# RWKV-7 heads of a diffusion trunk: the state chain of one turn interleaved with the token turns and gram blocks of the next

## The chip, the cores and the metric

The kernel runs on one core of a Trainium2 chip: TensorE (matmul), VectorE, ScalarE, GpSimd and SyncE (whose queue issues the DMAs) work in parallel and synchronise through semaphores. Matmuls write to PSUM, which has eight banks of 128 partitions x 512 fp32. The metric is the device time of one execution of the whole program in microseconds, lower is better.

## The reference

Two layers of a trunk over 256 latent and 256 context tokens, 1024 wide. Each layer projects its input, runs three token mixers (Mamba-2, RWKV-7, neighbourhood attention), merges them, and ends in a mixture of experts. The change is in the RWKV-7 mixer only: 16 heads of 64, both directions, context first, its final state the latent tokens' initial one. With `S` a 64 x 64 state per head:

```
w = -softplus(-(w0 + tanh(wl) @ w2)) - 0.5;  decay = exp(-exp(w))
a = sigmoid(a0 + al @ a2);  g = sigmoid(gl) @ g2
kk = unit(k * k_k);  k_dir = k * (1 + (a - 1) * k_a)
def step(S, inp):
    s_kk = S @ kk_t
    S = S * w_t - outer(s_kk, kk_t * a_t) + outer(v_t, k_t)
    return S, S @ r_t
y = y_forward + flip(y_backward)
out = (groupnorm(y) * ln_w + ln_b + sum(r * k_b * r_k) * v) * g
```

## The kernel before

`rwkv_heads` does this chunked. The 512 tokens are eight chunks of 64. The 1024 channels are done in eight turns of 128 channels (two heads `h`, on partition halves; both directions `z` together). `mix(b, c, ...)` is turn b; c is the next turn, whose features are prepared meanwhile. There is one `mix` for each engine, and each runs its own list in program order; the interleaving is written out by hand, and waits on counting semaphores tie the lists together (`hold` on TensorE is such a wait). Layer 0 needs all 512 output tokens (t0 = 0), layer 1 only the last 256: there gram blocks 1 and 3, `inside`, `across`, the mean, the variance and one of three projections are half as large.

A turn on TensorE is, in this order:

- `tokens`: matmuls with an identity turn the keys (two times), the left factor and v so that tokens lie on partitions; ScalarE copies them out of PSUM (`bkt`, `ag`, `vt`; semaphore `tok`). The bonus and the mean and variance of turn b-1 (`mean`, `variance`) stand between them.
- `gram`: blocks of 64 x 64 products of key and left features, masked; VectorE (`nevac`) or ScalarE (`gevac`) take them out, GpSimd masks some.
- `inverse`, stages 0 to 7: the inverse of (I - strictly lower part) in each chunk, by products of 64 x 64 blocks (`STAGES`: head, left, right, into, crossed, how it is taken out, PSUM bank). VectorE and ScalarE share the evacuations.
- `gram_times_v`, `apply_inverse`, `chunk_products` (M, N and R products), `inside`.
- `chain`: six sequential steps over the chunks. In each, TensorE multiplies the state by the chunk's transition (eight records), VectorE adds to it (L2435, `st0`, `st1`), and `across` adds the state's part of the output.

In turns 0 to 5, `filler(count)` places `count` of 24 matmuls of the projection for turn b+2 (k, v, then r; 128 x 512 each, recorded as two) between the groups; turns 6 and 7 have none. `projection_weights` on SyncE asks for the next weights when a projection is done (`proj`).

The features of turn c on VectorE: `shift_key` (L2319, L2321), `sums`, `centre`, `shift_rest` (L2326, L2328), `unit_key`, `key` (L2355), `away` (L2358), `key_sum` (L2361), `key_weigh`, `decayed` (L2367) and `decayed_left` (L2370), which multiply in decays that ScalarE's `decay_powers` makes (`exps`). `Steps.do` waits for its own instruction, `put` does not, `settle` waits for those put. Other lines: L2387 masks grams on VectorE, L2403, L2405, L2407 are its evacuations of the inverse, L2412, L2417, L2422 those of `apply_inverse`, M and N products, L2427 is `read_out` (rp), L2441 `centred`, L2445 to L2448 `out`. On ScalarE L2136 takes grams out, L2156 is `y_out` (yb), L2165 and L2167 are `root`. On GpSimd L2251 is `receptance`, L2258 `copy_receptance`, L2266 the masks. All 64-wide matmuls have the line of the helper `cell`, L1761; fillers are L1770, the bonus L1805, mean L1951, variance L1955.

## Time and profile before

| | |
|---|---|
| median of 3 runs | 4146.75 us (4141.01 to 4150.22) |
| the profiled execution | 4140.64 us, span 4138.9 us |
| granted TensorE clock, mean over the span | 0.956 |
| TensorE, VectorE, ScalarE, GpSimd busy | 90%, 38%, 25%, 16% |
| RWKV turns, layer 0 | about 918 to 1590 us of the span |
| RWKV turns, layer 1 | about 3016 to 3640 us |

Times in rows are microseconds from the span's start, unless marked ns. PE is TensorE, DVE VectorE, ACT ScalarE, POOL GpSimd. A row of a timeline gives start, length, engine, line, operation, tiles (out<-in), count, and in brackets how long the engine idled before it and for whom. "issue" is idle time for which the profile shows no cause. Windows give the length, then busy time and count of PE, PEld (weight load), DVE, ACT and POOL, the granted clock (1.00 is 2.4 GHz, 0.50 is 1.2 GHz), the DMA engines' busy share and GB/s. Rows of waits give total us, times, and the longest.

### The profile page before, as it was taken

The numbers are of one execution on the slowest core, as the hardware profiler recorded it, in microseconds if no ns is written. First come the engines' busy times: TensorE is split into PE (matmuls) and PEld (weight loads), VectorE is DVE, ScalarE is ACT, GpSimd is POOL, SyncE is SP. The second block draws the span as 40 slices with busy tenths as digits, with TensorE's granted clock in tenths as the row PEclk, the third lists the DMA queues.
The fourth block names the chain that finished last, engine by engine and source line by source line (L and its number), as shares of the span: only waits on it lengthen the run. The fifth ranks groups of instructions, "written<-read, shape, count | busy, mean of one in ns | idle before, by whom it ended". The sixth has DMA issues, their size and how long they took to land. (4 is left out here: it accounts for less than half of the span.)

```text
span 4138.9 us, 97532 instructions
## 1 busy us (share of the span) xinstructions
PE 3711.3 (90%) x44008; PEld 2344.1 (57%) x44008; DVE 1575.3 (38%) x2897; ACT 1040.4 (25%) x1817; POOL 656.7 (16%) x531
## 2 busy tenths in 40 slices
PE   7899998999988869999999598998989988798897
PEld 3454446446555655488877354656656666674332
DVE  3566304135555551143331146003255655422111
ACT  2211005124443441010000221104144444311001
POOL 0141102003333330010000002102023323200000
PEclk8999999999999999989999799999999999898999
DMA  4105312220001011379998310323300010147997
GB/s 182 61 26 182 128 61 52 102 60 26 21 25 27 5 44 42 123 271 380 384 382 318 133 61 21 112 90 84 98 22 26 26 27 6 44 158 310 403 403 282
DMA packets 300561, 539.03 MB, mean 130 GB/s; under 512 B 53552, under 2 KB 161344, under 8 KB 300016
## 3 DMA queue, kind: packets, MB, share of 16 engines
q1 hardware_dynamic: 288032, 489.06, 33.5%
q0 software_dynamic: 12112, 43.65, 2.9%
q8 instruction: 354, 5.80, 0.6%
q14 instruction: 63, 0.52, 0.0%
HBM read 514.77 MB, written 17.87 MB: 129 GB/s over the span
## 5 line engine op out<-in xcount | busy, mean ns | idle before, releaser
L1261 PE MATMUL bank<-sb_h,sb_ring 128*128 128x512 f32 (+1 forms) x1344 | 474.2, 512 | 9.6 <-DMA sb_ring<-w_branch 6.0
L1761 PE MATMUL bank<-inv 64*64 64x64 f32 x15104 | 356.5, 226 | 118.5 <-DVE inv L2407 26.4
L1761 PEld LDWEIGHTS bank<-inv 64*64 64x64 f32 x15104 | 314.3, 139 | 241.6 <-issue 239.2
L1261 PEld LDWEIGHTS bank<-sb_h,sb_ring 128*128 128x128 f32 x1344 | 254.4, 190 | 222.7 <-issue 196.4
L1770 PE MATMUL bank<-sb_h,sb_ring 128*128 128x512 f32 (+1 forms) x672 | 350.7, 616 | 6.6 <-DMA sb_ring<-w_in 4.1
L3199 PEld LDWEIGHTS bank<-xs,gu 128*128 128x128 f32 x3072 | 345.5, 192 | 8.6 <-issue 7.8
L3199 PE MATMUL bank<-xs,gu 128*128 128x96 f32 x3072 | 346.0, 275 | 1.1 <-issue 0.6
L784 PE MATMUL bank<-sb_h,sb_ring 128*128 128x512 f32 x512 | 232.4, 612 | 19.5 <-SPq L244 19.5
L2403 DVE COPY inv<-bank 128x512 f32<-128x512 f32 x144 | 99.6, 692 | 269.3 <-PE bank L1761 267.7
L784 PEld LDWEIGHTS bank<-sb_h,sb_ring 128*128 128x128 f32 x512 | 99.9, 197 | 139.2 <-issue 118.4
L2959 PE MATMUL bank<-gu,xs 128*64 128x512 f32 x768 | 169.7, 594 | 8.0 <-DMA gu<-moe_w_up 7.5
L1261 PE MATMUL bank<-sb_branch,sb_ring 128*128 128x512 f32 (+1 forms) x512 | 170.7, 486 | 0.0
L3213 PE MATMUL bank<-sb_ring,hid 128*96 128x512 f32 x384 | 167.5, 592 | 1.2 <-issue 1.2
L2142 ACT ACTIVATE inv<-bank 128x512 f32<-128x512 f32 x176 | 103.5, 597 | 237.3 <-PE bank L1761 237.3
L1497 DVE TENSOR_TENSOR sb_acc<-zs,bank 128x512 f32<-128x512 f32 (+1 forms) x16 | 8.9, 555 | 340.2 <-PE bank L1261 340.2
L1770 PEld LDWEIGHTS bank<-sb_h,sb_ring 128*128 128x128 f32 x672 | 107.7, 195 | 50.6 <-issue 25.9
L1261 PEld LDWEIGHTS bank<-sb_branch,sb_ring 128*128 128x128 f32 x512 | 97.0, 190 | 69.0 <-issue 60.9
L2266 POOL TENSOR_TENSOR gm<-gm,sb_consts 128x512 f32<-128x512 f32 (+1 forms) x96 | 124.9, 1330 | 0.0
L3102 DVE TENSOR_TENSOR hid<-hid,bank 128x192 f32<-128x192 f32 x16 | 5.7, 355 | 311.2 <-ACT hid L3154 311.2
L2959 PEld LDWEIGHTS bank<-gu,xs 128*64 128x64 f32 x768 | 53.4, 137 | 118.7 <-issue 99.7
L3213 PEld LDWEIGHTS bank<-sb_ring,hid 128*96 128x96 f32 x384 | 61.3, 163 | 95.7 <-issue 95.7
L1246 POOL TENSOR_TENSOR nabias<-nabias,sb_consts 128x1024 f32<-128x1024 f32 x16 | 38.4, 2399 | 486.1 <-DMA nabias<-na_bias 485.9
(423 smaller groups left out, 5815.5 us busy)
## 6 DMA issues: line engine op xcount, KB each, us to landing
sb_ring<-w_in SPq DMA_DIRECT2D x24, 2048.0 KB, 7.9
gu<-moe_w_gate SPq DMA_DIRECT2D x128, 384.0 KB, 8.2
gu<-moe_w_up SPq DMA_DIRECT2D x128, 384.0 KB, 9.8
sb_ring<-moe_w_down SPq DMA_DIRECT2D x96, 512.0 KB, 5.9
gu<-moe_w_gate SPq DMA_DIRECT2D x64, 768.0 KB, 14.0
gu<-moe_w_up SPq DMA_DIRECT2D x64, 768.0 KB, 14.9
sb_ring<-moe_w_down SPq DMA_DIRECT2D x32, 1024.0 KB, 14.9
sb_ring<-w_in SPq DMA_DIRECT2D x26, 1024.0 KB, 5.1
```

What stands on the lines that cost most here:

```text
L784: m = mm(k.bank[j], k.ring[:, h, kt, P * j:P * j + P], k.h[:, kt], start=kt == 0, stop=kt == KT - 1)
L1246: nc.gpsimd.tensor_tensor(dst, dst, mask, ALU.add).then_inc(s.added, 1)
L1261: mm = nc.tensor.matmul(out, left(kt), right(kt), start=kt == 0, stop=kt == KT - 1)
L1497: tt(k.acc[:, t, t0:], sg[:, t % 2, t0:], projs[0][t % 2][:, 0:n], ALU.mult).then_inc(s.merged, 1)
L1761: m = mm(k.bank[bank][H[to], at:at + w], left, right, start=start, stop=True, skip_group_check=True)
L1770: m = mm(k.bank[banks[j]][:, WHOLE[j]:], w[:, j, kt], k.h[:, kt, WHOLE[j]:], start=kt == 0, stop=kt == KT - 1)
L2142: ac(slot(h, into), eight(k.bank[bank]), ACT.Copy).then_inc(s.ev_a, 1)
L2266: tt(gm[:, h, j, chunks], gm[:, h, j, chunks], spread(mask(name, h), chunks.stop - chunks.start), ALU.mult).then_inc(s.masked, 1)
L2403: nc.vector.tensor_copy(dst, src).then_inc(s.ev_v, 1)
L2959: m = mm(wide[i][rows[e], :], xs[:, kt, rows[e]], cols[:, 512 * i:512 * i + 512], start=kt == 0, stop=kt == KT - 1)
L3199: m = mm(wide[j // 4][:, C * (j % 4):C * (j % 4) + C], w[:, P * j:P * j + P], xs[:, kt], start=kt == 0 and j % 4 == 0, stop=kt == KT - 1, ...
L3213: m = mm(outs[half][0:C], hid[:, r % 2, f], ws.down[d % ws.n_down][:, 0, 512 * half:512 * half + 512], start=f == 0, stop=f == HT - 1)
```

## The change

The chain of turn b is crossed with `tokens` and `gram` of turn c = b+1 (`crossing`): chain steps, key turns, left and value turns and the first gram block alternate on TensorE, then follow the other gram blocks with the mean and variance of b, and the bonus of c. A turn so begins with the inverse. Before turn 0 there is a `crossing` with no chain. Of the 24 fillers, six lie in the crossing; none is left between gram blocks. All features of c are now made between the inverse's stages and ahead of the chain's end: both keys move in front of stage 6, `away` and `key_sum` in front of `chunk_sums`, the decays between chain steps. `shift_rest` is split into `shift_sum` and `shift_mix`. VectorE's `finish` and `bonus` stand between the evacuations of stages 0 and 1. The PSUM banks of nearly all products are dealt out anew, and with them some of the counts waited for. On ScalarE `tokens`, two gram evacuations, `square` and `root` of b move to the end of turn b. The core of the diff:

```diff
     [[(0, "n1", "n0", "q0", 0, "copy", 2), (1, "n1", "n0", "q0", 1, "vcopy", 6)],
-     [(0, "n0", "n1", "q1", 0, "copy", 5), (1, "n0", "n1", "q1", 1, "vcopy", 3)]],
-    [[(0, "q1", "q0", "n0", 0, "copy", 1), (1, "q1", "q0", "n0", 1, "vcopy", 0)],
-     [(0, "q0", "q1", "n1", 0, "copy", 2), (1, "q0", "q1", "n1", 1, "vcopy", 3)],
...
-        KEY_BANKS, LEFT_BANKS, V_BANKS, BONUS_BANK = ((0, 4), (1, 6)), (0, 4), (1, 6), 2
-        GRAM_BANKS, TURNED_BANKS, OTHER_BANK = {0: (3, 5), 2: (2, 6), 1: (5, 1), 3: (0, 4)}, (0, 4), 1
-        M_BANKS, N_BANKS, R_BANKS, CHAIN_BANKS, Y_BANK = (2, 4), (0, 1), (3, 5), (4, 0), 2
+        KEY_BANKS, LEFT_BANKS, V_BANKS, BONUS_BANK = ((1, 6), (4, 5)), (1, 6), (4, 5), 3
+        GRAM_BANKS, TURNED_BANKS, OTHER_BANK = {0: (1, 6), 2: (2, 6), 1: (4, 0), 3: (5, 1)}, (4, 5), 0
+        RATE_BANKS, GATE_BANK, NORM_BANK, GTV_BANKS, P2_BANKS = (2, 0), 2, 0, (2, 0), ((1, 4), (3, 5))
+        M_BANKS, N_BANKS, R_BANKS, CHAIN_BANKS, Y_BANK, SUM_BANK = (2, 0), (1, 3), (4, 5), (0, 3), 2, 3
...
+            def gram_block(b, j, chunks):
+                free = {(0, 0): (s.tok, b(8, 5)), (0, 1): (s.tok, b(8, 6)), (2, 0): (s.tok, b(8, 8)), (2, 1): (s.nevac, b(6, 2)),
+                        (1, 0): (s.nevac, b(6, 3)), (1, 1): (s.nevac, b(6, 4)), (3, 0): (s.nevac, b(6, 5)), (3, 1): (s.nevac, b(6, 6))}
+                for c in chunks:
...
-            FIRST = {(0, 0): ("nevac", 6, 5), (0, 1): ("nevac", 6, 6), (1, 0): ("gevac", 6, 5), (1, 1): ("xready", 2, 1), (1, 2): ("xready", 2, 2),
...
+            def bonus(b, ended):
+                hold(s.bonus_in, b(1, 1))
+                if ended:
+                    hold(s.vlog, ended(1, 1))
+                mm(k.bank[BONUS_BANK], const(k, "headones"), ks[:], start=True, stop=True).then_inc(s.bonus_d, 1)
+
+            FIRST = {(0, 0): ("nevac", 6, 5), (0, 1): ("gevac", 6, 4), (1, 1): ("xready", 2, 1), (1, 2): ("xready", 2, 2),
...
-                    if (g, i) == (0, 1):
-                        hold(s.gevac, b(6, 3))
+                    if (g, i) == (1, 1):
+                        hold(s.gevac, b(6, 5))
                     if (g, i) == (1, 2):
                         hold(s.plus, b(2, 1))
                         hold(s.gevac, b(6, 6))
+                        hold(s.bvd, b(1, 1))
...
                                      (s.prod0, s.prod1)[h] if c == NC - 1 else None)
                     if i == 0 and filler:
-                        filler(1)
+                        filler(2)
...
+            def step(b, pos):
+                for z in range(2):
                     if pos > 1:
+                        hold((s.st0, s.st1)[z], b(6, pos - 1))
+                    for h in range(2):
+                        cell(CHAIN_BANKS[z], h, 0, 64, mt[z][H[h], ORDER64[z][pos]], state(z, pos)[H[h]], True, (s.ch0, s.ch1)[z])
+
+            def crossing(b, c, kept, filler):
+                if b:
+                    hold(s.g3in, b(4, 4))
+                    step(b, 1)
+                    filler(2)
+                    step(b, 2)
+                if c:
+                    hold(s.rawin, kept)
+                    key_turns(c, 0)
+                if b:
+                    step(b, 3)
+                    hold(s.rin, b(2, 2))
+                    for pos in range(1, 4):
                         for z in range(2):
                             across(z, pos)
-                for z in range(2):
-                    hold((s.st0, s.st1)[z], b(6, 6))
-                    across(z, 7, s.y_done if z else None)
+                if c:
+                    key_turns(c, 1)
+                if b:
+                    step(b, 4)
+                    for z in range(2):
+                        across(z, 4)
+                if c:
+                    left_turns(c)
+                if b:
+                    filler(2)
+                    step(b, 5)
+                    for z in range(2):
+                        across(z, 5)
+                if c:
+                    value_turns(c)
+                if b:
+                    step(b, 6)
+                    for z in range(2):
+                        across(z, 6)
+                if c:
+                    gram_block(c, 0, range(NC))
+                if b:
+                    for z in range(2):
+                        hold((s.st0, s.st1)[z], b(6, 6))
+                        across(z, 7, s.y_done if z else None)
+                if c:
+                    gram_turned(c)
+                    gram_other(c)
+                    if b:
+                        filler(2)
+                        mean(b)
+                    gram_block(c, 2, range(NC))
+                    hold(s.rdec, c(2, 2))
+                    gram_block(c, 1, out_chunks)
+                    if b:
+                        variance(b)
+                    gram_block(c, 3, out_chunks)
+                    bonus(c, b)
...
-                tokens(b, raws, ended, filler)
-                gram(b, ended, filler)
-                inverse(b, 0, filler)
+                inverse(b, 0)
+                filler(1)
                 inverse(b, 1, filler)
                 filler(1)
                 if c:
                     hold(s.low_in, c(32, 32))
                     hold(s.ev_a, b(N_EV_A, AFTER[0][1] + 1))
                     hold(s.ev_v, b(N_EV_V, AFTER[0][2] + 1))
-                    decay_and_rate(0, (0, 1))
+                    decay_and_rate(0, RATE_BANKS)
                 inverse(b, 2, filler)
                 filler(1)
                 if c:
                     hold(s.wa_in, c(4, 2))
-                    decay_and_rate(1, (0, 1))
-                inverse(b, 3, filler)
-                filler(1)
+                    decay_and_rate(1, RATE_BANKS)
+                inverse(b, 3)
+                filler(2)
...
                 apply_inverse(b)
                 filler(1)
                 chunk_products(b, filler)
-                filler(1)
                 inside(b)
-                filler(1)
-                chain(b)
-                assert at[0] == 3 * KT * project
+                crossing(b, c, b(3, 8) if project else 3 * TURNS, filler)
...
+            def bonus_bias(b):
                 act.wait_ge(s.bvd, b(1, 1))
                 ac(bv[:, t0:], bv[:, t0:], ACT.Identity, bias=ln[:, 1:2]).then_inc(s.bvr, 1)
...
-            def mix(b, c, at, ended, project):
-                whole, outs = slice(0, NC), slice(first_out, NC)
-                tokens(b, ended)
-                gram(b, 2, 14, whole)
-                gram(b, 1, 18, outs)
+            whole, outs = slice(0, NC), slice(first_out, NC)
+
+            def mix(b, c, at, project):
                 inverse(b, 0)
                 gram(b, 3, 22, outs)
                 inverse(b, 1)
+                bonus_bias(b)
                 if c:
                     keep_middle(c)
-                    decay_and_rate(0, c, (0, 1))
+                    decay_and_rate(0, c, RATE_BANKS)
                 inverse(b, 2)
                 if c:
                     key_square(c)
-                    decay_and_rate(1, c, (0, 1))
+                    decay_and_rate(1, c, RATE_BANKS)
                 inverse(b, 3)
                 if project:
                     keep(1, c, b(3, 7))
@@ -2197,9 +2226,15 @@
                 apply_inverse(b)
                 if c:
                     decay_powers(c)
+                    tokens(c)
+                y_out(b)
+                square(b)
                 if project:
                     keep(0, c, b(3, 9))
-                y_out(b)
+                if c:
+                    gram(c, 2, 14, whole)
+                    gram(c, 1, 18, outs)
+                root(b)
...
+                pool.wait_ge(s.shifted, c(3, 3))
...
+                if ended:
+                    pool.wait_ge(s.vb, 8 + ended(MIX_STEPS, 6))
...
+            def gram(b, m, ended):
                 for h in range(2):
-                    taken(4, slot(h, "n1"), GRAM_BANKS[0][h], mask("strict16", h))
-                taken(8, slot(0, "n0"), TURNED_BANKS[0], mask("strict16", 1))
-                taken(10, gm[:, 1, 0], OTHER_BANK, mask("strict", 0))
-                taken(8, slot(1, "n0"), TURNED_BANKS[1], mask("strict16", 0))
-                taken(4, gm[:, 0, 0], GRAM_BANKS[0][0], mask("strict", 0))
+                    taken(b, 4, slot(h, "n1"), GRAM_BANKS[0][h], mask("strict16", h))
+                taken(b, 8, slot(0, "n0"), TURNED_BANKS[0], mask("strict16", 1))
+                taken(b, 10, gm[:, 1, 0], OTHER_BANK, mask("strict", 0))
+                if ended:
+                    centred(m, ended)
+                taken(b, 8, slot(1, "n0"), TURNED_BANKS[1], mask("strict16", 0))
+                taken(b, 4, gm[:, 0, 0], GRAM_BANKS[0][0], mask("strict", 0))
 
             def inverse(b, g):
...
-            def mix(b, c, m, f, ahead):
+            def mix(b, c, m, f, before, ahead):
+                inverse(b, 0)
+                if before:
+                    finish(*before)
                 bonus(m, b)
                 m.settle()
                 if c:
                     columns(f, c, ahead)
-                gram(b)
-                inverse(b, 0)
...
                 inverse(b, 5)
                 if c:
-                    shift_rest(f, c, 2, 2, vv)
+                    key(f, c, 0)
+                    key(f, c, 1)
+                    shift_sum(f, c, 2)
                 inverse(b, 6)
                 if c:
-                    shift_rest(f, c, 3, 0, r)
+                    shift_mix(f, c, 2, 2, vv)
+                    shift_sum(f, c, 0)
                 inverse(b, 7)
                 if c:
+                    shift_mix(f, c, 3, 0, r)
                     unit_key(f, c)
                 apply_inverse(b)
                 if c:
-                    key(f, c, 0)
+                    f.settle()
+                    away(f, c, 0)
                 chunk_moves(b)
                 if c:
-                    key(f, c, 1)
+                    away(f, c, 1)
+                    key_sum(f, c)
+                chunk_sums(b)
+                if c:
                     f.settle()
-                chunk_sums(b)
+                    v.wait_ge(s.exps, c(1, 1))
+                    decayed(c, 0, 0)
+                chain(b, 1)
+                if c:
+                    decayed(c, 0, 1)
                 read_out(b, 0)
-                chain(b, 1)
+                chain(b, 2)
                 read_out(b, 1)
-                chain(b, 2)
                 if c:
-                    away(f, c, 0)
+                    decayed(c, 1, 0)
                 chain(b, 3)
                 if c:
-                    away(f, c, 1)
+                    decayed(c, 1, 1)
+                    decayed_left(c, 0)
                 chain(b, 4)
                 if c:
-                    key_sum(f, c)
-                    f.settle()
+                    decayed_left(c, 1)
                 chain(b, 5)
                 if c:
                     key_weigh(f, c)
                 chain(b, 6)
                 if c:
-                    v.wait_ge(s.exps, c(1, 1))
-                    decayed(c, 0, 0)
-                    decayed(c, 0, 1)
-                centred(m, b)
-                if c:
-                    decayed(c, 1, 0)
-                    decayed(c, 1, 1)
-                    decayed_left(c, 0)
-                    decayed_left(c, 1)
                     features_done(f, c)
                     f.end()
+                    gram(c, m, b)
+                else:
+                    centred(m, b)
 
             def finish(m, b, at):
```

## Rows read from the trace of the kernel before

**Rows 1.** The page of the profiled execution: span, and busy time by engine.

```profile
span 4138.9 us, 97532 instructions
...
PE 3711.3 (90%) x44008; PEld 2344.1 (57%) x44008; DVE 1575.3 (38%) x2897; ACT 1040.4 (25%) x1817; POOL 656.7 (16%) x531
```

**Rows 2.** Windows: stretch, length, busy time by engine, clock, DMA.

```profile
1084.80:1170.90 86.10, 77.98 (x2122) 51.21 (x2123) 48.63 (x82) 38.16 (x58) 27.52 (x21) 0.96 0.09 24
...
3249.70:3328.10 78.40, 71.13 (x1972) 49.18 (x1970) 44.70 (x81) 35.83 (x58) 25.18 (x21) 0.94 0.10 26
...
3250.00:3255.00 5.00, 4.52 (x111) 3.56 (x112) 3.74 (x7) 2.49 (x4) 1.38 (x2) 0.50 0.01 3
```

**Rows 3.** TensorE's waits, 1084.8 to 1426.2; the last row 3093.9 to 3485.9.

```profile
PE bank L1761 <- DVE inv L2407: 7.7, 4, 2.0
PE bank L1761 <- DVE rp L2427: 5.7, 4, 1.5
PE bank L1761 <- ACT gm L2136: 5.2, 4, 1.3
PE bank L1761 <- issue: 5.0, 4, 1.8
PE bank L1761 <- DVE bb L2367: 3.9, 4, 1.5
...
PE bank L1761 <- ACT gm L2136: 5.7, 5, 1.1
```

**Rows 4.** Timeline of TensorE, layer 0, around one chain.

```profile
1164.12 0.45 PE L1761 MATMUL bank<-inv 64*64 64x64 f32 x8
...
1170.91 0.52 PE L1761 MATMUL bank<-rp,inv 64*64 64x64 f32 x8 [0.29 <-DVE inv L2435]
1172.12 1.12 PE L1951 MATMUL bank<-yb,sb_consts 128*128 128x512 f32 x2 [0.69 <-ACT yb L2156]
```

**Rows 5.** Timeline of TensorE, layer 0, stages 6 and 7 of the inverse.

```profile
1228.10 1.16 PE L1761 MATMUL bank<-inv 64*64 64x64 f32 x64
1229.19 1.13 PE L1770 MATMUL bank<-sb_h,sb_ring 128*128 128x512 f32 x2
1232.36 1.99 PE L1761 MATMUL bank<-inv 64*64 64x64 f32 x64 [2.04 <-DVE inv L2407]
```

**Rows 6.** Timeline of TensorE, layer 1, around one chain.

```profile
3243.16 0.45 PE L1761 MATMUL bank<-inv 64*64 64x64 f32 x8
...
3249.13 1.29 PE L1761 MATMUL bank<-rp,inv 64*64 64x64 f32 x16
3250.90 1.22 PE L1951 MATMUL bank<-yb,sb_consts 128*128 128x256 f32 x2 [0.48 <-ACT yb L2156]
3252.05 3.94 PE L1761 MATMUL bank<-sb_consts,bb 64*64 64x64 f32 x128
```

**Rows 7.** Timeline of VectorE, layer 0, end of a chain.

```profile
1170.48 0.47 DVE L2435 SCALAR_TENSOR_TENSOR inv<-bank,gg,inv 128x64 f32<-128x64 f32 x2
1170.87 1.29 DVE L2367 TENSOR_TENSOR bb<-bb,sb_ring 128x512 f32<-128x512 f32 x2
```

**Rows 8.** Timeline of ScalarE, layer 0: the variance's Ln, a gram pair.

```profile
1179.81 0.69 ACT L2165 ACTIVATE inv<-bank,fixed 128x512 f32<-128x512 f32 x1 [1.58 <-PE bank L1955]
...
1190.53 1.08 ACT L2136 ACTIVATE gm<-bank 128x512 f32<-128x512 f32 x2 [4.17 <-PE bank L1761]
```

**Rows 9.** Two lines of VectorE over both layers: least, median, longest ns.

```profile
L2355 DVE TENSOR_TENSOR bb<-bb,rkv x32: 681/684/1549, 912.7 to 3553.3; 128x512 f32<-128x512 f32 x32
...
L2326 DVE TENSOR_TENSOR sb_ring<-sb_ring x32: 681/692/1384, 893.8 to 3542.9; 128x512 f32<-128x512 f32 x32
```

**Rows 10.** Timeline of TensorE, heads of turns 6 and 7, layer 0.

```profile
1437.96 0.81 PE L1761 MATMUL bank<-bb,cc 64*64 64x64 f32 x38 [0.78 <-ACT ag L2126]
1439.39 0.62 PE L1761 MATMUL bank<-bb,cc 64*64 64x64 f32 x25 [0.62 <-issue]
...
1519.68 0.92 PE L1761 MATMUL bank<-cc,bb 64*64 64x64 f32 x25 [4.80 <-issue]
```

161 lines of the change are left out of this document (64 added, 97 removed), and 25 rows, old and new, of the table STAGES.

## Prediction

> **What bounds the kernel now.** I read the share of busy time first: TensorE is busy 90% of the span [rows 1]. The windows then narrow this to the changed function, which runs once a layer: a filled turn takes 86.1 us in layer 0 and 78.4 us in layer 1, TensorE is busy for 78.0 and 71.1 of them and VectorE for 48.6 and 44.7, and TensorE's granted clock averages 0.96 and 0.94 [rows 2]. So time is won only where TensorE waits or runs at its lower clock. The waits name the places. Over four turns of layer 0, waits for inv L2407, rp L2427, gm L2136, bb L2367 and "issue" are 7.7, 5.7, 5.2, 3.9 and 5.0 us; in layer 1 the one for gm L2136 is 5.7 us over five turns [rows 3]. Last comes the order of time around one chain.
>
> In layer 0 the chain's first product starts at 1164.12 and its last ends at 1171.43: 7.3 us [rows 4]. It issues 48 records for the six steps and 56 across; at the pace of a full group (64 records, next instruction 1.09 us later: 1228.10 to 1229.19 [rows 5]) that is 1.8 us. So 5.5 us are lost in the alternation with VectorE. Then come 0.7 us for yb [rows 4] and 3.9 us in four turns, 1.0 each, for bb ahead of the second key turns [rows 3]. In layer 1: 3243.16 to 3250.42 is 7.3 us, of which 80 records need 1.4, so 5.9 lost, and 0.5 for yb; besides, the clock stands at 0.50 behind that idling, 1.2 GHz: 128 key records take 3.94 us against 2 x 1.16 at 2.4 GHz, and the mean's 1.22 are some 0.5 too long, in all 2.1 [rows 2, 5, 6].
>
> **The change, part by part.** All 24 fillers, all products and all evacuations of a turn stay; only their places and banks change. What counts is how much of the waiting goes, and what arises.
>
> *Removed, in a crossing between two filled turns.* The chain's loss (5.5 in layer 0, 5.9 in layer 1), the wait for yb (0.7, 0.5: `mean` now stands behind four groups and two fillers), the second key wait (1.0, 0), and the wait for the last masked gram, 1.3 and 1.1, since the first product of the inverse's second stage no longer waits for `gevac` 5 [rows 3]. In layer 1 also the lower clock's 2.1, since the gaps below are short and apart. Together 8.5 and 9.6.
>
> *Added, VectorE inside the crossing.* Back to back, a 512-wide operation comes 0.60 us after the last and a chain pair takes 0.39: 1170.48 to 1170.87, and 1.29 us for two that last 0.69 each [rows 7]. Between step 1 and the left turns VectorE has four chain pairs, five decays after the first, the sixth ahead of it, and two read-outs. VectorE starts some 0.48 behind a step's first product (1164.12 lasts 0.45 [rows 4]). Counted from step 1: step 2 behind two fillers at 2.3, chain 2 at 2.7, chain 3 behind a read-out and a decay at 4.3, the fourth decay done at 5.4, so the second key turns start at 5.5, where TensorE is ready at 4.4: 1.1. Step 4 comes at 6.6, chain 4 at 7.1, the sixth decay is done at 8.1, and the left turns wait from 6.9: 1.4. In layer 1 the fillers here are 256 wide, half as long, so chain 2 comes at 1.8, chain 3 at 3.2, the key turns at 4.4 and the left turns at 7.1: 1.6 and 1.5. The value turns and first gram block wait for nothing: ScalarE copies a pair in 1.1 us while two fillers run.
>
> *Added, the group mean's tail.* `bonus` waits for `vlog`, behind two gram evacuations (1.1 each) and the Ln (0.7) on ScalarE [rows 8]: 3.2 us with latency after the second gram block, of which the variance and the last block cover 2.1: about 0.9, and 1.0 in layer 1. The Exp and its table load then delay ScalarE, but `bonus` and the inverse's first product cover them.
>
> *Added, features inside the inverse.* Before, VectorE has two operations (L2326, L2328) between the evacuations of stages 5 and 6, and TensorE stands idle 2.04 us for the next, L2407 [rows 5]. Now there are three (two keys, one sum). A sum (L2326) lasts 0.68 to 1.38 us and a key (L2355) 0.68 to 1.55 [rows 9]; the long ones stand beside GpSimd's work, and here its late masks run. One such operation more: 1.4 later in layer 0, 1.0 in layer 1, where the masks are half as wide and end sooner. The bounds are 0 (all three at 0.68) and 1.6. What follows stage 6 has slack again: two short operations behind a filler.
>
> *Added, ahead of the chain.* `chunk_sums` (L2422) now waits behind `away` and `key_sum`, both beside GpSimd's `receptance`, where one key stood, so one operation of that length later, some 1.5 us. In layer 0 that hides under a filler, the R products and `inside`; in layer 1 the last two are half as long and two fillers have gone, so the chain starts 1.4 late (0 if the two run at 0.6).
>
> *Added, waits and instruction supply.* About eight more holds: an estimate of 0.5, between nothing and 8 times the 0.29 of the shortest wait in [rows 4]. And there are now two runs of 250 to 320 records without a filler. The trace does show gaps put down to "issue" in such runs: in filled turns four in 5.0 us, the longest 1.8; 0.62 in the unfilled head of turn 6; and 4.80 in turn 7's head [rows 3, 10]. Bounds: 0 and 9.6 a crossing; I take 1.0, nearest to one gap of the ordinary size. The Trainium skill, "Runtime: NRT & Kernel Launch", section Instruction fetch mechanics, says that fetching is hidden under the sequencer's issue pace; by it this term would be nil and the time some 14 us less. The 4.80 us row speaks against the rule, without proving a fetch.
>
> *Moved, costed at nothing.* `finish` and VectorE's `bonus`, some 3.5 us, now stand between the evacuations of stages 0 and 1 instead of ahead of the grams. Cover: the filler behind stage 0, stage 1's first product and two fillers, 4.3 us in all; gone, the difference would be a wait, and 1 us of it is easily missed, since bank 3 must be free (`bvd`) for stage 1's third product. GpSimd's off-diagonal copy now waits for the first step of `finish` (it shares a slot with the variance); its product comes in stage 2, some 5 us later. SyncE's queue keeps its order: the weights of the next projection follow each projection as before, and the last of the three now ends inside the crossing, a turn ahead of its use.
>
> Sums: layer 0, 8.5 - (1.1 + 1.4 + 0.9 + 1.4 + 0.5 + 1.0 = 6.3) = 2.2 won; layer 1, 9.6 - (1.6 + 1.5 + 1.0 + 1.0 + 1.4 + 0.5 + 1.0 = 8.0) = 1.6. There are five such crossings a layer: 11 + 8 = 19.
>
> *The others.* Turn 5 to 6: before, the head of turn 6 has no fillers and loses 0.8 for the left evacuation and twice some 0.6 to issue [rows 10] above the rest; now it has turn 5's. That adds 2.0 to each net, 4.2 and 3.6: 7.8 for both. Turn 6 to 7, without fillers, keeps the 4.8 stall, and nothing but the keys and blocks covers VectorE's operations: I take 1.1 a layer, about half of a filled crossing's net, 2.2 for both. The very first tokens lose seven fillers (they return in 5 to 6) and wait for copies instead: -2 a layer, -4. Total won: 19 + 7.8 + 2.2 - 4 = 25 us.
>
> The profiled execution took 4140.64 us (span 4138.9), 6 below the median 4146.75; the sum taken from it is 4116, and carried to the median **4122 us**.
>
> **Rivals.** (1) *More is hidden.* The mixed work keeps TensorE at 2.4 GHz throughout, also where layer 0 now dips once a turn (the group at 1232.36 takes 1.99 us against 1.16 [rows 5]; with the filler and the next group behind it some 1.8 us of loss), no issue gaps come, and the two decay waits halve: 2.2 + 1.8 + 1.0 + 1.3 = 6.3, and 1.6 + 1.0 + 1.5 + 0.7 (sums half as late) = 4.8, so 55.5 in ten crossings; 6 + 8 elsewhere: 69 won, 4078. For it: gaps get shorter everywhere in the crossing. Against: stage 6's gap grows to 3.4. (2) *The longer gap at stage 6 drops the clock every turn*, and layer 1 does not get all of its 2.1 back: 2 us in each of ten crossings: 20 of the 25 are gone, 4142. For it: the group behind the 2.04 us idling, 1232.36, runs at half pace. (3) *Slower, by one mechanism*: TensorE's instructions do not come fast enough in the two filler-free runs of a crossing, as at 1519.68 [rows 10]. With 3.5 us more in each of 14 crossings, 49 lost: 24 slower, 4171. It decides from 1.8 us more a crossing (25 / 14). Against it: the gaps in filled turns average 1.2 [rows 3]. (4) *Nothing changes*, since VectorE sets the pace: against it, VectorE is busy only 48.6 of 86.1 us [rows 2].
>
> **Chances and range.** Forecast (4102 to 4142) 0.43, rival 1 0.24, rival 2 0.13, rival 3 0.16, rival 4 0.04. A difference within 0.2%, 8 us, is what a measurement of this kernel cannot tell from none. Of rival 2 half lies within 8 us, 0.04 beyond it on the faster side and 0.03 on the slower; of the forecast's own range nearly all is faster. Faster 0.70, same 0.11, slower 0.19. The range 4070 to 4160 takes in the forecast, most of rival 1 and rival 2, and leaves out about 0.07 below and 0.12 above.
>
> **What would show it.** Right: a turn some 2 us shorter than in [rows 2], in either layer; rp L2427 and yb L2156 gone from what TensorE waits for; new waits for the decays (bb, cc) of 1.1 to 1.6 us, a wait for ScalarE's Ln ahead of `bonus`, L2407's grown to about 3.3. Layer 1's clock up from 0.94. Wrong: sums late in layer 0 too; "issue" over 2.5 us more a turn (rival 3); a clock under 0.93 (rival 2). If the masks do not meet the keys, or VectorE's waits overlap with each other, I am too cautious.

## The result, and the profile after

The changed kernel takes 4111.43 us (median of 4 runs, 4103.29 to 4113.05) against 4147.54 for the kernel before in the same measurement: ratio 0.9914, 95% interval 0.9898 to 0.9931, so 36 us won. The profiled executions have spans of 4138.9 [rows 1] and 4109.3 us, 29.6 apart.

Lines moved: the filler's products are L1771 (before L1770), all 64-wide products L1762 (L1761), the mean L1985 (L1951), the bonus L1835, the decays L2408 (bb) and L2411 (cc), the keys L2396 (L2355), the evacuations of the inverse's stages L2450 (L2407), L2446 and L2455. The page of the changed kernel, as in [rows 1]:

```profile
span 4109.3 us, 97594 instructions
...
PE 3676.8 (89%) x44008; PEld 2336.2 (57%) x44008; DVE 1602.1 (39%) x2897; ACT 1040.8 (25%) x1817; POOL 649.9 (16%) x531
```

The same number of products keeps TensorE busy for 34.5 us less. Windows of the changed kernel, each one filled turn, from the crossing's first key turns to the next ones; two of layer 0, then two of layer 1, columns as in [rows 2]:

```profile
996.72:1077.44 80.72, 72.78 (x2127) 48.85 (x2126) 50.51 (x81) 38.16 (x58) 27.17 (x21) 1.00 0.10 25
1158.91:1242.80 83.89, 75.52 (x2127) 51.00 (x2127) 49.67 (x80) 38.16 (x58) 27.16 (x21) 0.96 0.09 25
3080.59:3154.67 74.08, 65.00 (x1978) 45.78 (x1975) 47.36 (x81) 35.90 (x58) 24.27 (x21) 1.00 0.10 28
3228.01:3300.61 72.60, 65.08 (x1979) 45.99 (x1975) 46.70 (x81) 35.89 (x58) 24.77 (x21) 1.00 0.11 28
```

Against the five turns of a layer with the same marks before, a filled turn is on average 2.6 us shorter in layer 0 (84.9 to 82.4) and 4.5 in layer 1 (78.4 to 73.8). In layer 1 the clock is back at 1.00 from 0.94 [rows 2]. TensorE's waits in the changed kernel, four turns of layer 0 (1077.44 to 1408.56), as in [rows 3]:

```profile
PE bank L1762 <- issue: 15.5, 19, 1.7
PE bank L1762 <- DVE inv L2450: 10.5, 4, 2.9
PE bank L1762 <- DVE cc L2411: 4.4, 4, 1.1
PE bank L1762 <- DVE bb L2408: 2.7, 4, 0.7
PE bank L1835 <- ACT inv L2195: 0.3, 1, 0.3
```

and five turns of layer 1 (3080.59 to 3449.78):

```profile
PE bank L1762 <- issue: 21.7, 24, 1.8
PE bank L1762 <- DVE bb L2408: 6.4, 5, 1.3
PE bank L1762 <- DVE cc L2411: 5.5, 5, 1.1
PE bank L1762 <- DVE inv L2450: 4.3, 5, 0.9
PE bank L1762 <- DVE inv L2455: 1.5, 5, 0.3
PE bank L1835 <- ACT inv L2195: 1.4, 4, 0.4
PE bank L1771 <- issue: 1.1, 1, 1.1
PE bank L1762 <- DVE inv L2465: 0.7, 1, 0.7
```

The waits for rp, gm and yb are gone from both lists; those for cc and for ScalarE's Ln (L2195) are new, and in layer 1 that for bb too (in layer 0 bb was waited for before as well, 3.9 us [rows 3]), as forecast. What was not forecast stands first: issue is 3.9 us a turn in layer 0 (15.5 / 4, before 5.0 / 4 = 1.25) and 4.3 in layer 1 (before 7.3 us in five turns, 1.5). And a turn's idle time hardly falls (layer 0: 86.10 - 77.98 = 8.1 us in [rows 2], now 7.9 and 8.4; layer 1: 7.3, now 9.1 and 7.5): what falls is the busy time. One part of that is how a short group is counted: eight products show 0.40 to 0.52 us busy, where in a full group they take an eighth of 1.09 us. The other part is the clock. In layer 1 before, each turn has some 10 us at 1.2 GHz around its chain, such as this stretch (columns as in [rows 2]):

```profile
3246.20:3256.44 10.24, 9.38 (x187) 8.04 (x188) 7.57 (x19) 3.39 (x6) 1.38 (x2) 0.50 0.10 26
```

In the changed kernel's five turns of layer 1 nothing runs at 1.2 GHz. The chain in layer 0, on TensorE's timeline, now stands between full groups (before [rows 4]):

```profile
1243.85 0.40 PE L1762 MATMUL bank<-inv 64*64 64x64 f32 x8
1244.26 0.91 PE L1762 MATMUL bank<-rp,inv 64*64 64x64 f32 x24
1245.84 1.16 PE L1762 MATMUL bank<-sb_consts,bb 64*64 64x64 f32 x64 [0.67 <-DVE bb L2408]
1246.79 0.44 PE L1762 MATMUL bank<-inv 64*64 64x64 f32 x8
1247.03 0.43 PE L1762 MATMUL bank<-rp,inv 64*64 64x64 f32 x8
1248.57 1.16 PE L1762 MATMUL bank<-sb_consts,cc 64*64 64x64 f32 x64 [1.11 <-DVE cc L2411]
1249.66 1.98 PE L1771 MATMUL bank<-sb_h,sb_ring 128*128 128x512 f32 x4
...
1255.76 1.03 PE L1762 MATMUL bank<-bb,cc 64*64 64x64 f32 x53 [0.70 <-issue]
```

### The profile page after: what moved, and what is told of

The parts are those of the page before. It is cut to its first block and busy times, and to the rows that moved or that the text cites. A ratio compares the mean times of both kernels' runs of the same rounds, so it can differ in the third digit from the quotient of the medians.

```text
span 4109.3 us, 97594 instructions
## 1 busy us (share of the span) xinstructions
PE 3676.8 (89%) x44008; PEld 2336.2 (57%) x44008; DVE 1602.1 (39%) x2897; ACT 1040.8 (25%) x1817; POOL 649.9 (16%) x531
## 5 line engine op out<-in xcount | busy, mean ns | idle before, releaser
L1261 PE MATMUL bank<-sb_h,sb_ring 128*128 128x512 f32 (+1 forms) x1344 | 475.7, 513 | 10.1 <-DMA sb_ring<-w_branch 6.5
L1762 PEld LDWEIGHTS bank<-inv 64*64 64x64 f32 x15104 | 309.6, 141 | 207.0 <-issue 205.8
L1762 PE MATMUL bank<-inv 64*64 64x64 f32 x15104 | 347.3, 228 | 74.5 <-DVE inv L2450 28.7
L1261 PEld LDWEIGHTS bank<-sb_h,sb_ring 128*128 128x128 f32 x1344 | 255.5, 191 | 223.6 <-issue 196.4
L1771 PE MATMUL bank<-sb_h,sb_ring 128*128 128x512 f32 (+1 forms) x672 | 329.8, 605 | 7.2 <-DMA sb_ring<-w_in 3.9
L2446 DVE COPY inv<-bank 128x512 f32<-128x512 f32 x144 | 98.8, 691 | 218.0 <-PE bank L1762 217.1
L784 PEld LDWEIGHTS bank<-sb_h,sb_ring 128*128 128x128 f32 x512 | 100.4, 198 | 139.8 <-issue 119.1
L3010 PE MATMUL bank<-gu,xs 128*64 128x512 f32 x768 | 170.2, 595 | 10.8 <-DMA gu<-moe_w_up 10.3
L1771 PEld LDWEIGHTS bank<-sb_h,sb_ring 128*128 128x128 f32 x672 | 114.4, 195 | 79.0 <-issue 59.5
L1762 PE MATMUL bank<-cc,bb 64*64 64x64 f32 x4096 | 95.3, 229 | 26.5 <-issue 26.2
L2298 POOL TENSOR_TENSOR inv<-gm,sb_consts 128x512 f32<-128x512 f32 x64 | 88.6, 1395 | 178.5 <-PE bank L1762 166.5
```

The lines of the kernel that those rows point to most:

```text
L784: m = mm(k.bank[j], k.ring[:, h, kt, P * j:P * j + P], k.h[:, kt], start=kt == 0, stop=kt == KT - 1)
L1261: mm = nc.tensor.matmul(out, left(kt), right(kt), start=kt == 0, stop=kt == KT - 1)
L1762: m = mm(k.bank[bank][H[to], at:at + w], left, right, start=start, stop=True, skip_group_check=True)
L1771: m = mm(k.bank[banks[j]][:, WHOLE[j]:], w[:, j, kt], k.h[:, kt, WHOLE[j]:], start=kt == 0, stop=kt == KT - 1)
L2298: tt(slot(h, "o"), gm[:, h, 0], spread(const(k, name)), ALU.mult).then_inc(s.oready, 1)
L2446: nc.vector.tensor_copy(dst, src).then_inc(s.ev_v, 1)
```

## Where the time came from, by segments

Each run's span, cut at the same marks on TensorE's timeline (each layer's first key turns, each layer's last mean, and between the layers the first product on sq_first), in us. The two columns in which the changed function runs are "layer 0" and "layer 1":

```
kernel        to keys  layer 0  between  to keys 1  layer 1  end    span
before        920.9    664.6    767.8    665.2      615.9    504.6  4138.9
changed       922.0    651.7    769.1    670.3      586.5    509.7  4109.3
e1_apart      920.7    678.8    768.4    667.5      613.8    508.2  4157.5
e3_keys_late  921.7    637.1    767.5    665.8      596.6    506.6  4095.4
e5            922.1    639.3    769.2    665.7      589.6    508.6  4094.6
e7_apart_late 919.1    662.8    769.2    666.1      616.9    509.6  4143.6
e8_bunched    920.6    661.5    767.2    668.9      594.1    507.4  4119.7
e12_best      921.1    626.7    769.0    667.8      590.0    509.5  4084.2
```

Inside the function the change wins 12.9 and 29.4, 42.3; outside it 12.6 are missing. Each row is one execution, and the one of the kernel before was 6.9 us faster than its median (4140.64 against 4147.54), the changed one 0.4 (4111.08 against 4111.43), so about half of the 12.6 is the choice of execution. "To keys 1" lies between 665.1 and 670.6 over all runs though its code is the same, so its 5.1 are scatter. Of the end, 504.6 is the lowest of all runs and the others stand at 506.6 to 509.7. This does not go with the time that layer 1 takes: e1_apart and e7_apart_late, as long there as the kernel before, have 508.2 and 509.6. Nor does it go with the waits for the experts' weights: those for moe_w_up are 7.5 us before, 10.3 in the changed kernel and 7.4 in e5, whose end is 508.6. Its cause stays open.

## Experiments

In three sets (e1 to e4; e5 to e8; e9 to e12), each beside runs of the kernel before on the same chip. Ratios are to the kernel before.

**e1_apart.** The order on TensorE alone: the chain whole first, then tokens and grams. Orders on the other engines, banks and fillers stay as changed.

```
 def crossing(b, c, kept, filler):
     if b:
         step(b, 1); filler(2); step(b, 2); step(b, 3); ...
+        # steps 4 to 6 and all products across, here
     if c:
         key_turns(c, 0)
-    if b:
-        step(b, 3)
-        ...
         key_turns(c, 1)
         left_turns(c)
+        filler(2)
         value_turns(c)
         gram_block(c, 0, range(NC))
```

> The changed kernel, but TensorE runs the whole chain of turn b first and then the token turns and gram blocks of turn c; VectorE's and ScalarE's orders, all banks and the six fillers stay. Theory A (the gain comes from mixing the chain with other products): the chain again loses 4 to 5.5 us to VectorE in each of 14 crossings, less the 1.8 to 2.4 us of waits for the decays that the mixed order has; in layer 1 the granted clock falls again behind the chain and costs some 2 us more. About 3 us a turn in layer 0 and 5 in layer 1: 50 us over the changed kernel, near 4160. Theory B (the gain comes from the places of the mean, of gevac and of the fillers, and the mixing is nearly neutral): within 10 us of the changed kernel, near 4115.

Measured 4162.9 us, ratio 1.0038 [1.0024, 1.0052]: the mixing on TensorE is worth 0.0124 of the time, some 51 us, more than the whole gain. Both layers lose 27 us by the segments. So the rest of the change, taken together, costs.

**e2_gevac_back.** The first product of the inverse's second stage waits for the fifth gram evacuation again.

```
 FIRST = {(0, 0): ("nevac", 6, 5), (0, 1): ("gevac", 6, 4),
+         (1, 0): ("gevac", 6, 5),
          (1, 1): ("xready", 2, 1), ...
```

> The changed kernel, but the first product of the inverse's stage 1 again waits for gevac 5 (the copy of the last masked gram), as before the change. Theory A (the wait was worth its 1.1 to 1.3 us a turn, as the prediction has it): +0.9 to 1.2 us in each of 14 to 16 turns, 13 to 18 us slower than the changed kernel, near 4127. Theory B (a filler now stands between the stages, and ScalarE has copied by the time it ends): under 5 us slower, near 4113.

Measured 4107.6 us, 0.9903 [0.9888, 0.9917], the change's time. Over four turns this wait shows only 0.7 us. Taking the hold away won nothing by itself. The 1.3 and 1.1 us of [rows 3] went by the new order; that it is the filler now standing between stages 0 and 1 that covers the copy is argued, no run moved it alone.

**e3_keys_late.** The two keys go from between the evacuations of stages 5 and 6 to behind `unit_key`, in both layers.

```
                 inverse(b, 5)
                 if c:
-                    key(f, c, 0)
-                    key(f, c, 1)
                     shift_sum(f, c, 2)
                 ...
                     unit_key(f, c)
+                    key(f, c, 0)
+                    key(f, c, 1)
                 apply_inverse(b)
```

> The changed kernel, but the two key operations of VectorE stand behind unit_key, ahead of the evacuation of apply_inverse, instead of ahead of that of stage 6. Theory A (three operations beside GpSimd's masks are what TensorE waits 2.9 us for at stage 7 in layer 0, and the lower clock behind that is their cost too): the wait falls to some 1 us in layer 0 and nothing in layer 1; 2 to 3.5 us won a turn in layer 0 and 0.5 in layer 1: 15 to 24 us faster than the changed kernel, near 4092. Theory B (the work only moves: the keys then delay the copies behind apply_inverse and with them the chunk products): the wait for L2455 and L2465 takes the place, and the time stays within 6 us of 4111.

Measured 4093.9 us, 0.9866 [0.9852, 0.9880]: 18 us faster than the change. This is the version that beats both kernels.

**e5_late_layer0.** The same in layer 0 alone (`if c and l:` ahead of the early keys, `if c and not l:` ahead of the late ones).

> The two keys wait until behind unit_key in layer 0 only; in layer 1 they stay between the evacuations of stages 5 and 6. Theory A: the keys are slow only where GpSimd's late masks run beside them, which in layer 0 are twice as wide (two keys 3.42 us there, 1.40 in layer 1), so layer 0 wins what e3 won there (its turns end 14.6 us sooner) and layer 1 stays at 586.5 from its first key turns to the last mean, where e3 took 596.6. Then the time is some 10 us under e3's 4093.9: 4084. Theory B: e3's longer layer 1 is the scatter of one profile; then this is e3's time, 4091 to 4097. Theory C: moving the keys is what costs nothing anywhere and layer 1 gains from it too: over 4098.

Measured 4097.3 us, 0.9866 [0.9849, 0.9882]: e3's ratio. So theory B: no effect of the keys' place in layer 1 can be told, and one of up to some 9 us would not show between two such intervals. That e3's layer 1 is longer in its profile (596.6 against 586.5) proves nothing: cut at the same marks, e4's takes 597 us with its keys early. The reason stands on VectorE. One line's durations (least, median, longest ns), the keys in the changed kernel, layer 0, then layer 1:

```profile
L2396 DVE TENSOR_TENSOR bb<-bb,rkv x8: 881/1746/1752, 1135.4 to 1388.4; 128x512 f32<-128x512 f32 x8
...
L2396 DVE TENSOR_TENSOR bb<-bb,rkv x10: 678/680/814, 3137.2 to 3432.8; 128x512 f32<-128x512 f32 x10
```

and in e5, layer 0:

```profile
L2396 DVE TENSOR_TENSOR bb<-bb,rkv x8: 681/684/686, 1140.1 to 1383.0; 128x512 f32<-128x512 f32 x8
```

The changed kernel's timelines of VectorE and GpSimd show what runs at that time, and TensorE's what it costs:

```profile
1217.24 0.69 DVE L2446 COPY inv<-bank 128x512 f32<-128x512 f32 x1 [3.58 <-PE bank L1762]
...
1218.78 3.42 DVE L2396 TENSOR_TENSOR bb<-bb,rkv 128x512 f32<-128x512 f32 x2
1222.12 0.68 DVE L2365 TENSOR_TENSOR sb_ring<-sb_ring 128x512 f32<-128x512 f32 x1
1222.83 1.29 DVE L2450 TENSOR_TENSOR inv<-bank,sb_consts 128x512 f32<-128x512 f32 x2
```

```profile
1216.25 5.40 POOL L2303 TENSOR_TENSOR gm<-gm,sb_consts 128x512 f32<-128x512 f32 x4
```

```profile
1224.27 1.99 PE L1762 MATMUL bank<-inv 64*64 64x64 f32 x64 [2.89 <-DVE inv L2450]
```

GpSimd's four late masks (1216.25 to 1221.65) run beside all but the last half microsecond of the two keys. Taken away from them, the keys last 0.68 each (the one sum that stands there in e5 lasts 1.74 instead), and TensorE's wait for L2450 falls from 10.5 to 2.2 us in four turns (e5):

```profile
PE bank L1762 <- issue: 17.8, 20, 1.9
PE bank L1762 <- DVE cc L2411: 5.6, 5, 1.1
PE bank L1762 <- DVE bb L2408: 3.3, 5, 0.7
PE bank L1762 <- DVE inv L2450: 2.2, 4, 0.6
```

The windows of 1077 to 1409 give a clock of 0.98 with the keys early and 1.00 in e5: the group behind the 2.89 us of idling ran at half pace, 1.2 GHz (1.99 us for 64 products, 1.16 at 2.4 GHz). The Trainium skill, "GPSIMD Engine Reference", section Specifications, says that GpSimd's SBUF interfaces are shared with VectorE where VectorE's instruction has two SBUF inputs; the key has two, and the trace agrees with 1.75 against 0.68 us for the same operation.

**e7_apart_late.** e1 and e3 together.

> Chain whole and ahead of the tokens and grams, as in e1, and the keys late, as in e3, in both layers. Theory A: the mixing and the keys' place are independent: 4162.9 - 17.6 = 4145, the time of the kernel before, so that the change is one gain (mixing, some 52 us) and one loss (keys beside the masks, 16 to 18 us), and its other parts are worth nothing. Theory B: with the chain apart, VectorE's two keys ahead of apply_inverse make its evacuation and the chain's first sums late, and take half of that back: 4153 or more. Theory C: other parts of the change gain too (the features inside the inverse free VectorE in the crossing): under 4140.

Measured 4145.4 us, 0.9989 [0.9978, 1.0000]. The four kernels make a square:

```
                chain apart   chain mixed   mixing is worth
keys early      1.0038        0.9914        0.0124
keys late       0.9989        0.9866        0.0123
late is worth   0.0049        0.0048
```

Within the intervals (each time is known to about 0.0015) the two effects are independent: mixing wins 51 us and the early keys cost 20. All other parts of the change together are worth 0.0011, 5 us, and by e7's interval between 0 and 9. 51 - 20 + 5 = 36, the measured gain. That small rest is a difference of two larger things, which the square does not part: TensorE's issue, in 1085 to 1440, is 5.6 us before but 21.9 in e1 and 22.8 in e7 (18.8 in the changed kernel), so the growth of issue does not come from the mixing, and something else in the rest (the waits for gm, yb and the second keys that went) pays for it.

**e4_fill_runs.** Three single fillers move out of pairs and into the long runs of 64-wide products; all 24 stay.

```
-                    filler(2)
+                    filler(1)
                     step(b, 5)
...
                 if c:
+                    filler(1)
                     gram_turned(c)
                     gram_other(c)
                     if b:
-                        filler(2)
+                        filler(1)
                         mean(b)
                     gram_block(c, 2, range(NC))
+                    filler(1)
                     hold(s.rdec, c(2, 2))
```

> The changed kernel, with three of the crossing's six fillers moved: one from in front of step 5 to in front of gram_turned, and one from in front of the mean to between gram blocks 2 and 1, so that the two long runs of 64-wide products are cut in halves. Theory A (gaps put down to issue are a supply of instructions that runs dry in such runs, 2.6 us a turn more than before the change): half of it goes, 1.3 us in 12 crossings, 15 us faster than the changed kernel, near 4096. Theory B (the issue gaps are waits that the profile does not name, or slack that other waits take up): within 6 us of 4111, with the same idle time under another name.

Measured 4105.7 us, 0.9893 [0.9879, 0.9907]; the interval overlaps the change's, so the gain is not settled. Issue in 1077 to 1409 fell from 15.5 to 10.7 + 2.1 us.

**e6_late0_fill.** e4 and e5 together.

> Both: the keys late in layer 0, and the three fillers of e4 moved into the runs without one. Theory A: the two are independent, e4's 6 us come on top: 4078 if e5 is 4084. Theory B: e4's 6 us were the scatter of a measurement (its interval and that of the change overlap): the same as e5 within 3 us.

Measured 4094.2 us, 0.9860 [0.9843, 0.9877], the same as e5: theory B. Issue in layer 0's window fell from 17.8 to 13.1 + 1.9 us, too little to be measured in the whole.

**e8_bunched.** The opposite: the pair ahead of the mean joins that ahead of step 5 (`filler(4)` there, none at the mean).

> The opposite of e4: the two fillers ahead of the mean are moved to the two ahead of step 5, so that from step 5 to the end of the bonus no filler stands. Theory A (gaps put down to issue come where a run of 64-wide products is long): issue grows by 1 to 2 us a filled crossing, and 4117 to 4128 us. Theory B (such gaps come at certain places in the code whatever stands around them): issue stays at 3.9 and 4.3 us a turn, 4108 to 4114.

Measured 4133.1 us, 0.9956 [0.9943, 0.9970]: 17 to 22 us slower than the change for two fillers that stand some 8 us earlier. The mechanism is theory A's, but its size is larger than expected (4117 to 4128) and the list of waits did not grow as said (18.0 us of issue in 1077 to 1409, after 15.5). TensorE's timeline shows why:

```profile
1260.13 3.70 PE L1771 MATMUL bank<-sb_h,sb_ring 128*128 128x512 f32 x8
...
1266.83 0.33 PE L1762 MATMUL bank<-bb,cc 64*64 64x64 f32 x7
1269.92 1.86 PE L1762 MATMUL bank<-bb,cc 64*64 64x64 f32 x57 [2.76 <-issue]
1271.48 2.00 PE L1762 MATMUL bank<-cc,bb 64*64 64x64 f32 x32
```

One gap of 2.76 us in a crossing, and behind it half the clock (1.2 GHz): 57 products in 1.86 us where e10 below needs 1.08, the next 32 in 2.00 where it needs 1.14, and so with the mean behind them. Windows of e8, four turns of layer 0:

```profile
1077.00:1409.00 332.00, 296.01 (x8125) 198.07 (x8125) 189.91 (x309) 148.84 (x227) 105.79 (x82) 0.94 0.09 22
```

0.94, where the changed kernel has 0.98. So this gap cost about twice its length. The profiled execution is e8's fastest of six (4121.6), so what its slower ones lost beyond that is in no trace.

**What the gap waits for.** The DMA view lists a queue of the kind "instruction". For the changed kernel's turn 1077.44 to 1158.91 (packets, MB, share of the 16 engines):

```profile
q1 hardware_dynamic: 3536, 1.77, 8.1%
q8 instruction: 17, 0.28, 1.4%
```

17 transfers of 0.28 MB are 16 KB each, and for some 2127 products and as many weight loads they come to one per 250 TensorE instructions; over the whole span it is 354 transfers for 88016. Some of the gaps, beside the quarter microsecond in which such a transfer starts:

```
kernel    transfer in the quarter from   gap ends    later by   weights moving
changed   1087.50                        1089.94     2.4        no
changed   1151.75                        1154.15     2.4        no
changed   1169.50                        1172.13     2.6        no
changed   1179.75                        1182.26     2.5        yes
changed   1263.00                        1265.69     2.7        yes
e8        1094.00                        1096.59     2.6        yes
e8        1267.00                        1269.92     2.9        yes
before    1517.00                        1519.68     2.7        yes
```

The trace has the start and length of every such transfer. In the ten filled turns of the changed kernel 42 gaps of over 0.25 us are put down to issue. All 42 end 2.2 to 2.9 us after the start of a transfer of this queue, and 1.2 to 1.6 us after its end; of the 41 waits of such length for another engine in the same turns only three stand at that distance. In e8, at 1264.5 to 1267 the queue of weights is busy and none is there, and in 1267 to 1267.3 it comes, in the middle of a transfer of weights:

```profile
q1 hardware_dynamic: 988, 0.50, 82.8%
...
q1 hardware_dynamic: 212, 0.10, 115.6%
q8 instruction: 1, 0.02, 23.3%
```

The Trainium skill, "Runtime: NRT & Kernel Launch", section Instruction fetch mechanics, says that each sequencer fetches blocks of 16 KiB, 256 instructions, through a DMA queue of its own, and that this is mostly hidden. The trace agrees with the block's size and disagrees with the hiding: it shows 3.9 to 4.3 us of it a turn.

**e9_thin_weights and e10_bunched_thin.** Two kernels in which the later projections' transfers bring 64 KB in place of 512, so that the projections' results from turn 3 on are not the reference's: e9 is the changed kernel so cut, e10 is e8.

```
+                kts = slice(0, KT) if turn < 3 else slice(0, 1)
-                sp.dma_start(into[:, j], win[:, :, ...]).then_inc(done, 16)
+                sp.dma_start(into[:, j, kts], win[:, kts, ...]).then_inc(done, 16)
```

> The changed kernel with the weights of the later projections cut: from turn 3 on each transfer brings 64 KB (the first of eight tiles) instead of 512, so the projections' results are not the reference's; every instruction and wait stays. In the trace of the changed kernel each gap of TensorE put down to issue ends 2.4 to 2.8 us after the start of a 16 KB transfer on the DMA queue called instruction, and the longest (1.4 us, at 1182.26) stands where that transfer comes at the end of 0.72 MB of weights at 340 GB/s. Theory A: a fetch that falls into such a burst comes late; without bursts the gaps stay that long as the fetch itself takes (0.3 to 0.8 us), issue falls from 3.9 and 4.3 to 3 us a turn or less, 4100 to 4107 us. Theory B: the gaps come from the pace of fetches alone (one in 3.5 to 3.8 us at best) and not from the burst: issue and time stay, 4108 to 4114.

> e8 with the same cut of the weights. e8 took 4133.1, with one gap of 2.1 to 3.4 us put down to issue in each crossing and half the clock behind it. Theory A (the fetch is late behind the burst of weights): these gaps fall to 1 to 1.5 us, the clock stays at 1.00, and the time comes down to 4110 to 4120. Theory B (a long run of narrow products empties what was fetched, whatever the weights do): gaps and time stay, 4128 to 4136.

e9: 4108.6 us, 0.9902 [0.9885, 0.9919], not told apart from the change (theory B, though theory A's range ends 2 us below). A transfer of 16 KB takes 0.9 to 1.6 us in the changed kernel's trace, not the 0.3 to 0.8 of my expectation. e10: 4116.7 us, 0.9912 [0.9896, 0.9929] against e8's 0.9956: theory A, some 18 us come back. The same gap, ahead of the same 57 products, on TensorE's timeline of e10:

```profile
1256.04 0.33 PE L1763 MATMUL bank<-bb,cc 64*64 64x64 f32 x7
1257.49 1.08 PE L1763 MATMUL bank<-bb,cc 64*64 64x64 f32 x57 [1.12 <-issue]
```

2.76 us have become 1.12, and the next products run at full pace. The longest gaps of the other three crossings between 1077 and 1409 go from 3.43, 2.65 and 2.09 to 1.51, 0.82 and 1.54. The transfer ahead of the gap is not slower in e8, it starts later: its starts are 1260.15 and 1267.22, 7.1 us apart, in e10 1249.36 and 1254.56, 5.2 apart; in the 4 us ahead of the second of them 0.58 MB of weights start to move in e8 and 0.06 in e10. The clock of the four turns is 0.98 after 0.94 (not the 1.00 that was expected: dips remain around the wait for stage 6's evacuations). All issue of that window, however, only falls from 18.0 to 16.7 us, since other gaps grow, and the two profiled executions are 4.4 us apart (4119.7 and 4115.3) where the medians are 16.4 apart. So what is shown is this: a burst of weights makes a fetch start late and its gap long where the run is long, and without the bursts the time comes back; that these gaps are the whole of the 18 us is argued. A rest of 0.8 to 2.2 us a gap (e10, both layers) does not depend on weights.

**e11_weights_later.** SyncE's order: the small weights first, and the third projection's 512 KB only behind the bonus.

```
-                    for i, j in enumerate(STEP_ORDER):
+                    for i, j in enumerate(STEP_ORDER[:2]):
...
                 lora_weights(turn + 1)
+                if turn + 2 < TURNS:
+                    sp.wait_ge(s.proj, 3 * turn + 6 if turn else 3)
+                    sp.wait_ge(s.bonus_d, turn + 1)
+                    projection_weights(turn + 2, STEP_ORDER[2], w3, w_in[STEP_ORDER[2]])
```

> The changed kernel with SyncE's queue in another order: the small weights (wa, g) go first, and the third projection's 512 KB wait for the bonus at the end of the crossing. Nothing is left out. Theory A (fetches late behind the burst): no burst inside the crossing, so the 1.3 to 1.4 us gaps in it fall as in e9; the burst now stands beside the inverse's first stages, where a filler follows each group, so it costs less there: 4100 to 4108. Theory B: the burst costs the same wherever it stands, 4108 to 4114. Theory C: it meets the narrow products of stages 0 and 1 and costs more there: over 4114.

Measured 4114.7 us, 0.9911 [0.9894, 0.9928]: no gain, and e9 says that there is none to get. With pairs of fillers in place, no cost of the burst can be told in the changed kernel.

**e12_best.** e6 and e11 together.

> Keys late in layer 0 (e5), three fillers moved into the runs without one (e6), and the third weights behind the bonus (e11). Theory A: what e11 wins over the change comes on top of e6's 4094.2: 4083 to 4091. Theory B: with the fillers spread no gap is long enough to be lost to a burst any more: the same as e6, 4091 to 4097.

Measured 4091.6 us, 0.9865 [0.9846, 0.9884]: the same as e3, e5 and e6, though its one profile has the shortest span, 4084.2. Theory B. The late keys are the whole of what was found beyond the change.

## Why the prediction was right, and where it was not

The time, 4111, lies in the range and inside the likeliest case's own (4102 to 4142), 11 us under the forecast. That it came so near is in part luck: in the profiled pair the function itself won 42.3 us where 25 were forecast, and the 12.6 lost outside it were in no term. The ten filled crossings won 35.5 us for a forecast of 19, nearly all of the difference in layer 1. The steps, one by one, a filled crossing in layer 0 / layer 1:

*Removed, 8.5 / 9.6 us.* The waits for yb and gm, those between the chain's steps (L2435 before, none now) and layer 1's lower clock went as said; the chain's loss has no row of its own after the change, its size is taken over from the prediction. The reason given for gm was wrong (e2).

*Waits for the decays, forecast 1.1 + 1.4 / 1.6 + 1.5.* Measured 0.7 + 1.1 / 1.3 + 1.1. VectorE's order and its 0.60 us a piece [rows 7] gave places and sizes within 0.4 us.

*The group mean's tail, 0.9 / 1.0.* Measured 0.1 / 0.3 (the Ln's wait over all turns). ScalarE finished its gram pairs earlier against the second block than I had it.

*Features inside the inverse, +1.4 / +1.0.* Against the kernel before, the wait grew by 0.7 (1.9 to 2.6 a turn) and fell by 0.4 (1.3 to 0.9). I gave the masks half the effect in layer 1; there they are over before the keys start. In layer 0 most of the keys meet them fully, 1.75 us each, beyond the 1.55 of [rows 9]. But comparing with before hid the choice that mattered: e3 and e5 show that the change's own place for the keys costs 20 us in all, since without it the wait and the dip of the clock that the kernel before already had [rows 5] would have gone too. I had priced the growth of the wait, and not the possibility of ending it.

*Sums late in layer 1, 1.4.* Measured 0.14 (0.7 once in five turns). What it was built on did come: `key_sum` beside `receptance` took 1.75 us in each of the five turns, 0.69 before. But the evacuation behind it was late for TensorE only once in five turns, by half of what was forecast. The slack there was mis-sized.

*Holds, 0.5.* Nothing shows.

*Issue, +1.0.* Measured +2.6 / +2.9 a turn. This is the term mis-sized most. It does not come with the mixing, since e1 and e7 have as much of it. I had passed by its cause: of the gaps of the kernel before, those at 1439.39 and 1519.68 [rows 10] follow instruction transfers too (the latter is in the table).

The terms as measured, with the removed ones as forecast: layer 0, 8.5 - (0.7 + 1.1 + 0.1 + 0.7 + 2.6) = 3.3, where the marks say 2.6; layer 1, 9.6 - (1.3 + 1.1 + 0.3 - 0.4 + 0.1 + 2.9) = 4.3, where they say 4.5. The forecast said 2.2 and 1.6. So layer 0 was right with errors that cancel; in layer 1 the features, the sums and the mean's tail together were 3.4 us too dear, and issue 1.9 too cheap.

*Rivals.* Rival 1 (more is hidden, 4078) had the direction from the forecast, but not by its mechanisms: layer 0 still dips, issue grew, and the two decay waits are 1.8 of 2.5 and 2.4 of 3.1 us, not half. Layer 1's 2.4 GHz stood in the forecast already. Rival 2 is refuted as put: stage 6's wait grew in layer 0 and the group behind it still runs at half pace, as before, while layer 1's clock came back whole. Rival 3 came nearer than the time tells: it asked for 1.8 us more a crossing beyond the 1.0 charged, and 1.6 to 1.9 came; the other terms paid for it. e8 is that rival made real.

*The other turns.* Forecast 7.8 + 2.2 - 4 = 6 us for both layers. Measured, the segments less five filled turns: 12.9 - 12.8 and 29.4 - 22.7, together 6.8. The sum fits and its parts do not (0.1 and 6.7, where about 3 and 3 were forecast), so this agreement is luck.

## What to carry to other kernels

Fill a serial chain with independent full groups of the next iteration: what it frees is not only idle time but also the tails of short groups. Before moving an operation with two SBUF inputs on VectorE, look at what GpSimd runs at that time, and price its place against every other free place, not against the old kernel. Do not let TensorE's runs of narrow products grow (e8), and keep bursts of weights away from any run that must be long (e10). Cutting the runs further than the change does lowered issue (e4, e6), but won no time that could be measured.

## What the runs showed of the hardware

TensorE's instructions arrive in transfers of 16 KB, one per some 250 of them, through the same DMA engines as the data. In runs of 64-wide products 128 instructions (64 products and 64 weight loads) take 1.09 us [rows 5], so 256 are used up in 2.2 us, while the closest two such transfers in the changed kernel's filled turns start 3.3 us apart (others near that: 3.5 at 1179.92 and 1183.43, 3.7 at 1087.71 and 1091.41). One filler takes 1.13 us for four instructions (two records and their weight loads), so it gives the supply time. That the pace of the fetches sets the remaining gaps is argued from these distances; what starts a fetch, and whether it could start sooner, stays open, and products with fewer instructions were not tried.
